# Two-block transformer kernel: the split stationaries of three products placed at six distances from the ring of split weights

## The reference

```
p = rms_norm(x, mix_norm_g) @ w_in                      # 2048 x 5136
x = x + mixer(p) @ w_mix_out                            # 2048 x 2048
x = x + attention(h @ w_xq, rms_norm(mem) @ w_xkv) @ w_xo
x = x + (silu(conv(h @ w_gate)) * (h @ w_up)) @ w_down  # 2048 x 5632, twice, and back
x = rms_norm(x, final_norm_g)
x = x + gate * post_norm(mixers(modulate(norm(x)) @ w_in_2) @ w_o_2)
x = x + gate * post_norm(square(relu(h @ w_up_2)) @ w_down_2)   # 2048 x 8192 and back
```

## Time and profile before

| | |
|---|---|
| time, median of 2 runs | 2786.89 us (2786.67 and 2787.12) |
| span of the profiled execution | 2785.1 us |
| TensorE matmul, busy | 2725.2 us, 13302 instructions |
| VectorE, busy | 1772.1 us |
| ScalarE, busy | 1324.0 us |
| granted TensorE clock, mean | 0.993 |
| HBM, mean over the span | 207 GB/s |

### The profile page before, as it was taken

The page is one execution under the profiler, slowest core; times in us unless marked ns, Lnnn a source line. Parts: engine busy times, 40 slices in busy tenths (PEclk is TensorE's granted clock), DMA queues, the critical chain, the costliest instruction groups (busy, mean ns, idle before and its releaser), DMA issues.

```text
span 2785.1 us, 34787 instructions
## 1 busy us (share of the span) xinstructions
PE 2725.2 (98%) x13302; PEld 2329.5 (84%) x13302; DVE 1772.1 (64%) x2025; ACT 1324.0 (48%) x1679; POOL 169.5 (6%) x132
## 2 busy tenths in 40 slices
PE   8999999999999999999999999998989999999998
PEld 8999988888888888888888799887868888888887
DVE  4477488776578888765555564547775756645455
ACT  5555444454445454434455454446455344344443
POOL 0001620000000000000000002720000000000000
PEclk9999999999999999999999999999999999999999
DMA  8554068887477777775555556640755866755553
GB/s 284 164 170 131 1 242 275 290 278 261 164 259 273 273 279 272 274 257 182 194 182 200 181 188 204 200 151 1 259 180 197 280 204 238 261 189 177 191 185 132
DMA packets 293266, 579.60 MB, mean 208 GB/s; under 512 B 9168, under 2 KB 46192, under 8 KB 292112
## 3 DMA queue, kind: packets, MB, share of 16 engines
q1 hardware_dynamic: 291296, 566.08, 60.4%
q0 software_dynamic: 1120, 8.57, 0.8%
q10 hardware_dynamic: 720, 3.15, 0.3%
HBM read 575.66 MB, written 2.10 MB: 207 GB/s over the span
## 4 chain that ended last, share of the span: by engine, by line
PE 95%; DVE 3%; ACT 1%; issue 1%; DMA 0%; SPq 0%; POOL 0%; DVEq 0%; ACTq 0%
PE GP L1006 28%; PE GP L1008 28%; PE GP L1007 28%; PE TA L959 2%; PE TB L959 2%; PE TB L607 1%; PE TB L426 1%; PE GP L401 0%; PE TA L1375 0%; DVE wlo L1960 0%; PE GP L1216 0%; PE TA L1216 0%; PE GP L1203 0%; DMA x<-in_x 0%; DVE x L2402 0%
## 5 line engine op out<-in xcount | busy, mean ns | idle before, releaser
L1960 DVE TENSOR_TENSOR wlo<-raw,whi 128x1024 fp32r<-128x1024 f32 (+2 forms) x904 | 1088.2, 1217 | 812.2 <-ACT whi L1468 803.2
L1468 ACT CAST whi<-raw 128x1024 fp32r<-128x1024 f32 (+2 forms) x904 | 923.7, 1029 | 1170.8 <-PE GP L1008 1109.5
L1006 PE MATMUL GP<-whi,hhi 128*128 128x512 f32 (+2 forms) x1792 | 689.9, 385 | 1.9 <-issue 1.4
L1008 PE MATMUL GP<-whi,hlo 128*128 128x512 f32 (+2 forms) x1792 | 681.6, 380 | 0.0
L1007 PE MATMUL GP<-wlo,hhi 128*128 128x512 f32 (+2 forms) x1792 | 680.8, 380 | 0.0
L1006 PEld LDWEIGHTS GP<-whi,hhi 128*128 128x128 f32 x1792 | 338.1, 189 | 52.2 <-issue 3.3
L1008 PEld LDWEIGHTS GP<-whi,hlo 128*128 128x128 f32 x1792 | 337.8, 188 | 52.0
L1007 PEld LDWEIGHTS GP<-wlo,hhi 128*128 128x128 f32 x1792 | 338.3, 189 | 50.5 <-issue 1.0
L1006 PE MATMUL GP<-whi,bhi 128*128 128x512 f32 x704 | 277.0, 393 | 0.2 <-DVE blo L2021 0.2
L1948 DVE SCALAR_TENSOR_TENSOR ada_acc<-raw,csig,ada_acc 128x512 f32<-128x512 f32 x360 | 270.3, 751 | 10.2
L1008 PE MATMUL GP<-whi,blo 128*128 128x512 f32 x704 | 274.6, 390 | 0.0
(11 more groups left out here) (437 smaller groups left out, 2578.2 us busy)
## 6 DMA issues: line engine op xcount, KB each, us to landing
raw<-in_w_up SPq DMA_DIRECT2D x108, 1024.0 KB, 5.4
raw<-in_w_down SPq DMA_DIRECT2D x108, 1024.0 KB, 5.1
raw<-in_w_ada SPq DMA_DIRECT2D x96, 1024.0 KB, 5.2
raw<-in_w_gate SPq DMA_DIRECT2D x44, 1024.0 KB, 5.3
raw<-in_w_in SPq DMA_DIRECT2D x48, 856.0 KB, 4.7
raw<-in_w_xkv SPq DMA_DIRECT2D x32, 1024.0 KB, 5.7
raw<-in_w_in SPq DMA_DIRECT2D x24, 1024.0 KB, 5.0
raw<-in_w_in SPq DMA_DIRECT2D x24, 864.0 KB, 4.7
```

The source lines that it names most:

```text
L1006: pe.matmul(o, ahi[:, kt, t], whi[r][:, k, 0:q.width], start=first, stop=False)
L1008: m = pe.matmul(o, alo[:, kt, t], whi[r][:, k, 0:q.width], start=False, stop=last)
L1468: nc.scalar.copy(whi[(2 * g + s) % NRING][:, :, 0:q.width], raw[j % NSLOT][:, 2 * s:2 * s + 2, 0:q.width])\
L1960: TTo(wlo[r][:, :, 0:q.width], raw[j % NSLOT][:, 2 * s:2 * s + 2, 0:q.width], whi[r][:, :, 0:q.width].bitcast(F32), ALU.subtract).then_inc ...
```

## The change

`level` takes a second argument, a number of bytes past the ring's remainder. `mhi` moves to 32 bytes past it and `mlo` to 64, `bhi` to 128 and `blo` to 256, `f2hi` to 96 and `f2lo` to 384. `flo` and the tiles allocated behind these (`square`, `tok`, `ft`, `fsg`, `tok2`, `fq2`, `gpb1`, `dg1`) move along, `flo` to 256 bytes past the remainder. The last address in use rises from 227456 to 227840 of 229368. No instruction is added, removed or reordered.

```
-        def level(at):
-            return at + (ring0 - at) % 4096
+        def level(at, past=0):
+            return at + (ring0 + past - at) % 4096
...
         ar = Arena(); ar.at = level(arena0 + 4 * NH * 2 * D)
-        mhi = ar("mhi", [P, KT, T], F32R); mlo = ar("mlo", [P, KT, T], F32R)
+        ar.at = level(ar.at, 32)
+        mhi = ar("mhi", [P, KT, T], F32R)
+        ar.at = level(ar.at, 64)
+        mlo = ar("mlo", [P, KT, T], F32R)
...
         ar = Arena(); ar.at = level(arena0)
-        bhi = ar("bhi", [P, KT, T], F32R); blo = ar("blo", [P, KT, T], F32R)
+        ar.at = level(ar.at, 128)
+        bhi = ar("bhi", [P, KT, T], F32R)
+        ar.at = level(ar.at, 256)
+        blo = ar("blo", [P, KT, T], F32R)
...
         ar.at = level(ar.at)
-        f2hi = ar("f2hi", [P, 16, T], F32R); f2lo = ar("f2lo", [P, 16, T], F32R)
+        ar.at = level(ar.at, 96)
+        f2hi = ar("f2hi", [P, 16, T], F32R)
+        ar.at = level(ar.at, 384)
+        f2lo = ar("f2lo", [P, 16, T], F32R)
```

## The result

The changed kernel takes 2807.64 us (2807.55 and 2807.72) against 2786.89: the ratio is 1.0074, with a 95% interval of 1.0058 to 1.009. It is slower by 20.8 us, which is 0.7%. That is not the forecast of no change, and it lies inside the range (2776 to 2808) by 0.4 us.

A forecast was written before the change was run, and what follows sets the result against it. TensorE was taken as the bound, its time being matmuls times the step between starts. All terms were priced at 0: 2785.1 us span + 0, plus 1.8 us from span to median, gives 2786.9, said as 2787; range 2776 to 2808.

The forecast's parts named there:

- The bound and the control: TensorE, busy 98% of the span, sets the time; the unmoved `hhi` and `hlo` groups should keep 390 or 391 ns.
- The 4768 matmuls and 4.8 us for each nanosecond: Matmuls with a moved stationary number 4768, so each nanosecond on their step is 4.8 us, 0.17%.
- I take 0, the value of rows 7 and 8: Step change for moved stationaries set at 0, from float32 matmuls (275 against 276 ns) and transposes (273 against 272).
- the second rival: Load and stream of `whi` or `wlo`: level is good, a skew costs 1 to 13.5 ns a step; chance 0.16.
- The bound of 13.5 ns: Upper end of loss per step: longest unwaited step 0.24 us, behind transposes, against 226.5 ns; 64 us over 4768.
- Only what happens inside 512 bytes is open: Stationary-to-stream distances at multiples of 512 bytes show even groups and steps, so coarse distance doesn't matter; all six new distances are inside.
- the third rival: Change idle because memory is interleaved in 16 or 32 byte pieces: 2787 us, inside the 0.76 for no change.
- A load may become 38 ns longer before it shows: Weight loads under TensorE's matmuls: a load takes 188 ns inside a 226.5 ns step, leaving 38 ns of slack.
- The first rival: The 11.5 ns in each moved matmul's step are a load-stream collision a skew removes: 55 us faster, 2732; chance 0.08.

The follow-up runs named there:

- e9_low_ring: Changed kernel with `wlo` 128 bytes further from `whi`, `hhi` and the levelled tiles back at multiples of 256 from `whi`: 2832.35 us, ratio 1.0155.
- e11_unlevelled: Kernel before without its three calls of `level`; memory, feed-forward and second-net tiles lie 3616 bytes past the ring's remainder, down1 at 0/32 (high/low): 2820.38 us, ratio 1.0115.
- e10_both_low: Changed kernel with `wlo` and every low stationary (`hlo`, `mlo`, `blo`, `flo`, `f2lo`) 128 bytes further, the high ones at 0: 2822.91 us, ratio 1.0119.
- e6_scan_b: Changed kernel with high and low equal: memory 192/192, feed-forward 160/160, down1 224/224, second feed-forward 64/64 bytes: 2818.71 us, ratio 1.0118.

## Why the prediction was half right

**The bound and the control held.** TensorE's steps set the time, as read from the earlier trace rows: 23.5 us more in steps gave 20.8 in the span, and the 2.7 us between them are within what runs of one kernel differ by. The 4768 matmuls and 4.8 us for each nanosecond were right. The groups of `hhi` and `hlo` stayed where they were (390 for `hlo`, a step of 227.2) and made the reading certain within one trace.

**The step that failed is "I take 0, the value of rows 7 and 8".** These rows are float32 matmuls of 128 columns. The prediction had noted that they stream at half the rate and that a collision which needs the full rate could be hidden; it then let them set the value all the same. In float32r the same 32 bytes (0/32, 32/32) cost 6.1 to 6.5 ns a step; in float32 the pair `flat` against the ring, 32 bytes off, has 275 ns against 276, and its steps are 112 ns at the median in both sets of line 1203. The term was mis-sized by 4.9 ns on the mean of 4768 (23.5 us), and the kernel came out by the second rival, which had 0.16. Whether it is the type that made these rows blind isn't shown: they differ in the columns too, and float32r with 428 or 432 columns doesn't pay either at 128 bytes (`e9_low_ring`).

**That the range held is luck.** It took the second rival in up to 4.4 ns a step, and the mean rise was 4.9. By the steps alone the time would be 2786.9 + 23.5 = 2810.4 us, outside; the 2.7 us that the span didn't show brought it to 2807.6, under the edge of 2808. The choice of distances helped as well: `blo` and `flo` went to 256, which costs nothing by itself; with all moved tiles 32 bytes past a multiple of 256, as in `e11_unlevelled`, the kernel loses 33.5 us.

**The bound of 13.5 ns was read from the wrong rows.** The step of 0.24 us in the earlier trace rows isn't the one behind the transposes but the first of the next three matmuls. The one behind them is 0.32 us, with no idle time listed:

```profile
702.94 0.47 PE L1006 MATMUL GP<-whi,hhi 128*128 128x512 f32 x1
...
703.26 0.39 PE L1007 MATMUL GP<-wlo,hhi 128*128 128x512 f32 x1
```

The kernel before has 97 such steps, 306 to 319 ns. As the longest step without a wait they would have given a far wider bound, so the 13.5 ns had no ground. It did hold for the means: no product rose by more than 7.2 ns (96/96), and one line of one product by 12.4 (down1 at 0/32, line 1006 of `e11_unlevelled`).

**"Only what happens inside 512 bytes is open" was right, and could have been tighter.** The period is 256. The trace of before couldn't tell, since no float32r pair in it is at an odd multiple of 256. So `flo` and `blo`, at 256, were moved in name only, as the third rival had it for pieces of 16 or 32 bytes; the change was idle for one product and a third of the loads of another.

**"A load may become 38 ns longer before it shows" missed the form.** The loads stay at 187 to 189 ns in all runs, but for 192 with the high tile where only the low one is off by 128 or 384, and the step grows. The slack beneath a load was no protection here.

**The page.** The steps with 512 columns grow by 2 to 7 ns in 227 with the distance between load and stream. The Trainium skill, page "TensorE: Matmul & The Clock Gate", section "Step-by-step: what each phase is for", says that loading the next weights doesn't steal read bandwidth from the running matmul since each has its port. For float32 with 128 columns at 32 bytes the trace agrees, and so it does for float32r with 428 and 432 columns at 128 bytes (195 to 196 ns with and without). For float32r with 512 columns, seven distances modulo 256 speak against it: a load that took nothing from a stream could not make the step depend on the distance between the two. There the measurement decides.

**The first rival** (the 11.5 ns over 215 are a collision that a skew removes) found no distance whose mean is under 226.7. Whether the 11.5 ns are a collision too stays open: in `e10_both_low` steps of 224 ns exist, between longer ones.

## What to carry to other kernels

In float32r products with 512 columns whose stationary changes with every matmul, keep stationary and stream a multiple of 256 bytes apart in the partition: it cost nothing here, and leaving it out cost 1.2%. When rows are to bound an effect of timing between two readers, take rows of the same data type, rate and number of columns, or don't let them set the value. And keep part of the tiles unmoved in such a trial: their groups in the same trace are a better control than another run.

## What the runs showed of the hardware

- The mean step of a float32r matmul with 512 columns and a load each depends on the distance between its operands modulo 256 bytes: 227 ns at 0, 229 at 192, 230 to 234 at all others tried (multiples of 32).
- With 428 or 432 columns it doesn't, as far as tried: with `wlo` 128 bytes off, 194.8 and 195.6 ns against 195.1 and 195.9.
- Absolute addresses don't count (96 bytes on ring and stationaries: 1.0006). Moving one of the two streams costs as moving a stationary does (231 to 233 ns at 128 bytes).
- At equal distances steps can alternate, 236 and 231 ns at 64/64: a step goes with the one before it.
- Kernels with the same instructions can differ by a microsecond or more in how TensorE's clock stood behind the delta rule: granted 0.66 before, 1.00 in the changed kernel and 0.74 in `e6_scan_b`, over the same five microseconds.
